# One product of high and low float32r parts: from block by block to term by term

## The reference, cut to what matters

```
def swiglu(x, w_gate, w_up, w_down):
    return (jax.nn.silu(x @ w_gate) * (x @ w_up)) @ w_down
```

## Time and profile before

| | |
|---|---|
| median of three runs | 1109.17 us (1108.94 to 1109.27) |
| the profiled execution, its own time | 1111.79 us |
| its span, first to last instruction | 1109.7 us |
| TensorE busy | 1100.6 us, 99% of the span |
| weight loads busy (they overlap matmuls) | 984.7 us, 89% |
| VectorE busy | 776.2 us, 70% |
| ScalarE busy | 534.9 us, 48% |
| mean granted TensorE clock | 0.998 |

### The profile page before, as it was taken

One profiled execution on the slowest core, in us unless ns is written; L12 is line 12 of the kernel. 1 busy time (PEld: TensorE's weight loads), 2 busy tenths in 40 slices (PEclk: granted clock), 3 DMA queues, 4 the chain that ended last, 5 costly groups with the idle time before them and its releaser, 6 DMA issues.

```text
span 1109.7 us, 18347 instructions
## 1 busy us (share of the span) xinstructions
PE 1100.6 (99%) x6944; PEld 984.7 (89%) x6944; DVE 776.2 (70%) x1274; ACT 534.9 (48%) x921; POOL 33.5 (3%) x50
## 2 busy tenths in 40 slices
PE   9999999999999999999999999999999999999997
PEld 7999999988888888888898888888999999998886
DVE  6799999853348588774884865548799999963326
ACT  7355555642225477543463554435455555552222
POOL 0100000000002011010000000000000000000000
PEclk9999999999999999999999999999999999999999
DMA  7533333453323223342244262141233333363302
GB/s 227 190 115 115 115 104 107 128 182 98 101 66 99 73 86 83 99 152 76 76 151 135 65 182 62 53 133 58 76 115 115 113 103 109 115 194 107 98 19 76
DMA packets 33595, 121.30 MB, mean 109 GB/s; under 512 B 3900, under 2 KB 3916, under 8 KB 33264
## 3 DMA queue, kind: packets, MB, share of 16 engines
q1 hardware_dynamic: 30528, 109.07, 31.8%
q0 software_dynamic: 2992, 11.19, 3.2%
HBM read 118.13 MB, written 2.11 MB: 108 GB/s over the span
## 4 chain that ended last, share of the span: by engine, by line
PE 98%; DVE 1%; DMA 0%; issue 0%; ACT 0%; DVEq 0%
PE ps L539 20%; PE ps L541 20%; PE ps L540 20%; PE ps L621 10%; PE ps L623 10%; PE ps L622 10%; PE ps L562 1%; PE ps L824 1%; PE ps L845 1%; PE ps L912 1%; PE ps L896 1%; PE ps L817 0%; PE ps L816 0%; DMA raw<-in_units 0%; PE ps L1008 0%
## 5 line engine op out<-in xcount | busy, mean ns | idle before, releaser
L1615 DVE TENSOR_TENSOR wlo<-raw,whi 128x1024 fp32r<-128x1024 f32 x114 | 140.7, 1240 | 158.5 <-ACT whi L1074 157.4
L1074 ACT ACTIVATE whi<-raw 128x1024 fp32r<-128x1024 f32 (+1 forms) x131 | 134.3, 1032 | 135.2 <-PE ps L541 125.3
L539 PE MATMUL ps<-whi,hhi 128*128 128x512 f32 x480 | 187.8, 391 | 0.0
L541 PE MATMUL ps<-whi,hlo 128*128 128x512 f32 x480 | 186.9, 389 | 0.0
L540 PE MATMUL ps<-wlo,hhi 128*128 128x512 f32 x480 | 186.8, 389 | 0.0
L539 PE MATMUL ps<-xth,whi 128*128 128x512 f32 (+1 forms) x404 | 140.0, 347 | 0.0
L540 PE MATMUL ps<-xtl,whi 128*128 128x512 f32 (+1 forms) x404 | 137.8, 341 | 0.0
L541 PEld LDWEIGHTS ps<-whi,hlo 128*128 128x128 f32 x480 | 90.1, 188 | 18.9
L539 PEld LDWEIGHTS ps<-whi,hhi 128*128 128x128 f32 x480 | 90.1, 188 | 18.4 <-ACT km L1074 0.3
L540 PEld LDWEIGHTS ps<-wlo,hhi 128*128 128x128 f32 x480 | 90.1, 188 | 18.2
L541 PE MATMUL ps<-xth,wlo 128*128 128x512 f32 (+1 forms) x244 | 93.7, 384 | 0.0
(11 more groups left out here) (261 smaller groups left out, 2747.8 us busy)
## 6 DMA issues: line engine op xcount, KB each, us to landing
raw<-in_units SPq DMA_DIRECT2D x204, 512.0 KB, 3.7
xn<-in_x POOLq DMA_DIRECT2D x4, 512.0 KB, 7.8
gb<-in_ln_g POOLq DMA_DIRECT2D x4, 512.0 KB, 3.8
gb<-in_ln_b POOLq DMA_DIRECT2D x4, 512.0 KB, 5.3
wb<-in_bias_by_key POOLq DMA_DIRECT2D x8, 256.0 KB, 3.0
out<-xn SPq DMA_DIRECT2D x8, 256.0 KB, 2.1
gsp<-g_rows POOLq DMA_DIRECT2D x1, 1024.0 KB, 4.9
memn<-in_mem_cols POOLq DMA_DIRECT2D x1, 1024.0 KB, 5.8
```

The costliest lines, as they stand in the source:

```text
L539: mm(dst, lh, rh, start=start, stop=False)
L541: return mm(dst, ll, rh, start=False, stop=stop)
L1074: return nc.scalar.activation(*a, **k)
L1615: v.tensor_tensor(low_of(c)[:, :], raw[c % RAW][:, :], whi[c % SPL][:, :].bitcast(F32), ALU.subtract).then_inc(lo_done, 1)
```

## The change

The two loops inside `fast_part` change places. Before, for each block of K the three terms follow one another; after, each term runs over the four blocks of K before the next term begins. The 12 matmuls, their operands, the destination, the first matmul's clearing start and the signal on the last matmul are the same. Nothing outside the function changes.

```
             def fast_part(dst, wh, wl, xh, xl, start=False):
 
-                for k in range(KT // 2):
-                    c = slice(k * P, (k + 1) * P)
-                    mm(dst, wh[:, c], xh[:, k, :], start=start and k == 0, stop=False, skip_group_check=True)
-                    mm(dst, wh[:, c], xl[:, k, :], start=False, stop=False, skip_group_check=True)
-                    last = mm(dst, wl[:, c], xh[:, k, :], start=False, stop=k == KT // 2 - 1, skip_group_check=True)
+                for term, (w, x) in enumerate(((wh, xh), (wh, xl), (wl, xh))):
+                    for k in range(KT // 2):
+                        last = mm(dst, w[:, k * P:(k + 1) * P], x[:, k, :], start=start and term + k == 0,
+                                  stop=term == 2 and k == KT // 2 - 1, skip_group_check=True)
                 return last
```

## The result

The change makes the kernel slower: 1112.85 us (median of six runs, 1112.60 to 1113.64) against 1109.16 (six runs, 1108.82 to 1109.67). The ratio is 1.0033, 95% interval 1.0023 to 1.0043, so 3.7 us, with 2.6 to 4.8 in the interval. The forecast was 1109.2, no change, with a range of 1106.8 to 1112.0. The profiled execution took 1113.15 us itself.

The account below looks back on a forecast made before the run. The prediction took TensorE's matmul starts, 0.1133 us apart in the fast tiles, as the bound. All terms summed to 0, so the forecast stayed at the median 1109.17, rounded 1109.2 us, range 1106.8 to 1112.0.

Parts of the forecast that it names:

- Loads and repetition: TensorE's weight loads in the fast products: every matmul loads anyway, so giving up repeated high weights costs 0.
- Waits, signals and other engines: Heads and ends of products: waits and signals stay put, VectorE has 18.7 us of slack a stretch; cost 0.
- Steady rate by the distance modulo 128: Fast products: stream-to-load distance modulo 128 bytes sets the steady matmul rate; the new order keeps 64, so 0 ns a matmul.
- The six new kinds of pairs: Per product, three low-x streams over high loads and three high-x streams over low loads; taken at 0 ns a matmul.
- the settling: At x3 and x7, stream settling after both operands change places: 0.04 us a tile stays, -1.4 to +1.4 us overall.
- the keys' excess: Matmuls on the memory's keys, same shape, run at 0.120 us each, 6.7 ns more than in the fast products.
- the pairs: Stream-and-load pairs over all 3024 matmuls: taken as 0, bounded by +20.2 us and -14.5 us.
- The closing sentence: Prediction's caveat: the modulo-128 regularity may be only part of what decides, its rows all coming from the old order.
- Settling at each change of term: Slower rival: each passage to low x or low weights within a product unsettles the stream, +10.1 us, 1119.3; chance 0.06.
- new pairs at a slow rate: Slower rival: six new pairs a product run at 0.120, +10.1 us, 1119.3; chance 0.06, lost reuse included.
- long runs that stream faster: Faster rival: fewer changes of moving tensor within a product speed the stream, -10.9 us, 1098.3; chance 0.07 for faster streams.
- its smaller form: Smaller form of the faster rival: only the excess at x3 and x7 vanishes, 1107.8 us, within the 0.2%.

Follow-up runs that it names:

- e1: Changed kernel (term by term) with x3 and its weights placed 64 bytes higher, like the other products: 1108.32 us, ratio 0.9988 to the kernel before.
- e2: Kernel before (block by block) with x3 and its weights placed 64 bytes higher, like the other products: 1107.55 us, ratio 0.9983.
- e5: Kernel before with x3 alone 64 bytes higher, its weights left, so stream and weights lie 0 apart modulo 128: 1111.37 us, ratio 1.0019.
- e11: Kernel before with low weights of all seven fast products moved to lie like the high ones modulo 256: 1120.33 us, ratio 1.0097.
- e10: Kernel before with only x3's low weights moved by 128 bytes, to lie like its high ones: 1110.35 us, ratio 1.0011.
- e7: Kernel before, reordered: high weights by high and low x in each block, then low weights for all four blocks: 1112.63 us, ratio 1.0031.
- e13: Changed kernel (term by term) with all low weights moved to lie like the high ones modulo 256: 1120.30 us, ratio 1.0099 to the kernel before.
- e9: Kernel before, reordered: term by term over two blocks of K, then over the other two: 1110.70 us, ratio 1.0011.
- e6: Kernel before, reordered within each block: high by high, low weights by high x, high weights by low x: 1109.70 us, ratio 1.0004.

## Why the prediction was wrong

**Loads and repetition: right.** 6944 loads, none saved before. The rule cited from the Trainium skill (TensorE: Matmul & The Clock Gate, Step-by-step: what each phase is for), by which weights loaded once could serve several matmuls, has no hold here: e1, without repeated weights, and e2, with them, have the same tile of 9.52.

**Waits, signals and other engines: right.** The busy time of VectorE and ScalarE is as before and TensorE has no idle time in the stretches. A tile that e1 and e2 shorten by the places alone, with the same waits, leaves the waits nothing to explain.

**Steady rate by the distance modulo 128: right as far as it went.** The six new kinds of pairs run at 0.1133 wherever the stream is settled, and distance 0 was slow over the 12 matmuls of e5. But the distance does not set the rate by itself: at one distance of 64 the runs have 0.1133 and 0.118, by what went before, and by whether high and low weights lie alike modulo 256 (e11).

**The step that failed: the settling.** The prediction had "The settling at x3 and x7 stays, perhaps longer or shorter as it meets another sequence: from 0 to twice its 0.04 us". The place was right, and so was the cause, the change of both places at x3 and x7 (e1, e2). The size of this term was not. It measured 0.127 us a tile, 0.11 in x3 and x7 and 0.02 at the next product's start, three times the old value and beyond my upper bound. The difference of 0.087 times 36 tiles is 3.1 us, which the longer stretches show as 3.2. Behind the size stood a premise that the prediction did not test, that a stream settles by itself within a few matmuls. e10, e7 and e11 show that it need not: it stayed unsettled for 12, 24 and 72. The bound had no row behind it: the old trace had one value, from the old order, and "twice" was a guess. A bound from its rows was at hand. If the unsettled state lasts through x3 and x7, then at the keys' excess 24 matmuls x 6.7 ns = 0.16 us a tile, less the 0.04, times 36, give +4.3 us. If it lasts through the tile, the bound is the +20.2 us that the prediction had for the pairs, and left out of this term. The closing sentence had the weakness in view, that fast and slow rows all come "from the old rhythm of three", but neither range nor chances made room for it.

**The rivals.** Settling at each change of term did not happen: four matmuls on either side of a passage take 0.45 or 0.46 where the stream is settled (e1). (One reading against that rival was off: five of the seven products begin without excess, not six, since x7 has some of it too, 1.38 us.) Nor did new pairs at a slow rate, nor long runs that stream faster: e1 and e2 are alike. In its smaller form the last one, "the excess at x3 and x7 vanishes", came out the other way round.

The prediction kept the slower rivals against a rule of the Trainium skill (SBUF — State Buffer, Who interferes with whom) that TensorE's two read ports are independent and it never waits on anyone. Here the same 84 matmuls and loads take 9.52, 9.65, 9.86 or 9.89 us by addresses and order alone. e11 moves only low weights, which the loads read, and the stream goes from 0.1133 to 0.118: for float32r streams with a load each, loads and stream are not independent. That TensorE never waits on another engine, the other half of the rule, is not contradicted: the tiles of a trace agree to within 0.01 us.

**Still open.** Where in TensorE or its memory the two meet isn't visible. Not explained are why an unsettled stream lasts, why x3 settles in e11 and e13 without a passage, why the rows at 512 columns are the other way round (0.227 at distance 0, 0.233 at 64), and what keeps 0.1133 from the 0.109 of the transposes.

## What to carry to other kernels

When a stream of matmuls is the bound and each matmul loads its own weights, read starts over whole products, and look for stretches at a second rate: where operands change places modulo 128 bytes, moving a buffer by 64 bytes was worth more here (e2, -0.17%) than any order of the matmuls that was tried. An excess that is seen in one order only is no measure of it in another; for an upper bound, let it last until something in the kernel is shown to end it. A test in which the suspected cause is absent (e1) tells the order's own cost from what the order does to another cost.

## What the hardware showed that I had not expected

A matmul of 256 columns in float32r has two rates at the same addresses, 0.1133 and 0.118 us, depending on its history, and the slower one lasted for 72 matmuls of a tile in e11. At a distance of 64 modulo 128 between stream and weights the fast rate is to be had; at 0 (0.119) and at 32 (0.118) no settled stretch appeared. The slow state of distance 64 mostly ended after the loads had passed to low weights and back to high ones, where these lie at different places modulo 256: after some three matmuls at x3 in the block order, after six (e9) or nine (e6) in others, and only after 24 where the passage to low weights came at matmul 9 of each product. x3 in e11 and e13 left it without such a passage.
